# Attention heads of a fused decoder step: the rotated part of the scores on the two 64-row halves of the array by turns, a query tile's keys spread over two banks, no zero-padded key copies

## What is computed

```python
q = (c_q @ w_q_b).reshape(B, T, MLA_HEADS, QK_NOPE + QK_ROPE)      # 128 + 64 per head
q_pe = rope(q[..., QK_NOPE:], pos)
s = einsum('bqhc,bsc->bhqs', ql, c_kv) + einsum('bqhr,bsr->bhqs', qp, k_pe)
s = where(key_pos <= q_pos, s * ATTN_SCALE, NEG_INF)
p = softmax(s, axis=-1)
o = einsum('bhqs,bsc->bqhc', p, c_kv)
```

## Time and profile before

| | |
|---|---|
| runs of the kernel | 3501.75, 3492.95, 3504.45 us; median 3501.75 |
| the profiled execution | 3500.34 us, its span 3498.5 us |
| mean granted TensorE clock | 0.966 of full speed |
| TensorE busy in the array | 94% of the span, 26364 matmul records |
| weight loads | 84% |
| VectorE, ScalarE, GpSimd | 52%, 38%, 35% |

### The profile page before, as it was taken

One profiled execution on the slowest core, in us unless ns is written; L12 is line 12 of the kernel. 1 busy time (PEld: TensorE's weight loads), 2 busy tenths in 40 slices (PEclk: granted clock), 3 DMA queues, 4 the chain that ended last, 5 costly groups with the idle time before them and its releaser, 6 DMA issues.

```text
span 3498.5 us, 72361 instructions
## 1 busy us (share of the span) xinstructions
PE 3303.9 (94%) x26364; PEld 2948.1 (84%) x26364; DVE 1826.5 (52%) x3142; ACT 1345.1 (38%) x2810; POOL 1214.3 (35%) x847
## 2 busy tenths in 40 slices
PE   9999999999999999999999888888889999999998
PEld 6676766678899999997899877777778899999998
DVE  3454545213644377866203567666732464447785
ACT  2232323431454444322214455556521154453332
POOL 0000000010466677731223222223213066677771
PEclk9999999999999999999999989989978999999999
DMA  3121210630344554432223101100052045454442
GB/s 106 52 76 57 58 58 17 198 117 1 95 157 157 165 166 136 136 107 76 74 74 108 68 13 44 32 26 26 18 147 85 13 130 158 158 180 136 136 145 84
DMA packets 303577, 331.50 MB, mean 95 GB/s; under 512 B 54350, under 2 KB 285825, under 8 KB 303138
## 3 DMA queue, kind: packets, MB, share of 16 engines
q1 hardware_dynamic: 297346, 309.17, 27.9%
q0 software_dynamic: 6048, 19.73, 1.8%
HBM read 232.57 MB, written 116.69 MB: 100 GB/s over the span
## 4 chain that ended last, share of the span: by engine, by line
PE 60%; PEld 6%; DVE 5%; issue 4%; POOL 3%; ACT 2%; DMA 1%; SPq 0%; ACTq 0%; DVEq 0%; PEldq 0%; POOLq 0%
PE bank L615 58%; PEld bank L615 6%; PE bank L623 2%; POOL wloA L1953 1%; POOL arena L1953 1%; POOL wloS L1953 1%; DVE arena L3363 1%; DVE hT L3429 1%; SPq L1586 0%; ACT hT L2627 0%; DVE arena L3380 0%; DVE arena L2877 0%; DMA arena<-arena 0%; ACT arena L2177 0%; DVE arena L3067 0%
## 5 line engine op out<-in xcount | busy, mean ns | idle before, releaser
L615 PE MATMUL bank<-arena 128*128 128x268 f32 (+20 forms) x8302 | 1162.8, 333 | 77.9 <-ACT arena L2177 25.2
L615 PEld LDWEIGHTS bank<-arena 128*128 128x128 f32 (+7 forms) x8302 | 878.9, 178 | 339.7 <-issue 113.8
L1953 POOL TENSOR_TENSOR arena<-arena 128x512 f32<-128x512 f32 x120 | 165.7, 1381 | 1213.4 <-DMA arena<-in_ffn_w_up 766.9
L2177 ACT COPY arena<-bank 128x512 f32<-128x512 f32 (+14 forms) x557 | 252.6, 487 | 816.4 <-PE bank L615 590.9
L2357 ACT ACTIVATE whiS<-arena 128x512 fp32r<-128x512 f32 x180 | 113.0, 628 | 407.1 <-POOL arena L1953 393.9
L1953 POOL TENSOR_TENSOR wloA<-arena,whiA 128x512 fp32r<-128x512 f32 x180 | 262.4, 1471 | 0.4 <-ACT whiA L2354 0.4
L1953 POOL TENSOR_TENSOR wloS<-arena,whiS 128x512 fp32r<-128x512 f32 x180 | 238.9, 1341 | 49.1 <-ACT whiS L2357 49.1
L3229 DVE TENSOR_TENSOR hT<-hT,bank 128x536 f32<-128x536 f32 x280 | 197.4, 706 | 82.4 <-PE bank L615 82.0
L615 PE MATMUL bank<-hiT,whiS 128*128 128x268 f32 x768 | 199.9, 289 | 7.3 <-DVE loT L3071 3.7
L623 PE MATMUL bank<-table,arena 128*128 128x128 f32 (+5 forms) x1354 | 171.6, 268 | 26.1 <-DMA arena<-in_x_prompt 7.2
L3076 DVE TENSOR_TENSOR arena<-std,bank 128x268 f32<-128x268 f32 x192 | 80.4, 432 | 215.7 <-PE bank L615 209.3
(11 more groups left out here) (297 smaller groups left out, 8093.9 us busy)
## 6 DMA issues: line engine op xcount, KB each, us to landing
u_scratch<-arena SPq DMA_DIRECT2D x480, 134.0 KB, 1.8
arena<-in_ffn_w_up SPq DMA_DIRECT2D x64, 512.0 KB, 4.2
arena<-u_scratch SPq DMA_DIRECT2D x56, 536.0 KB, 5.1
arena<-in_ffn_w_down SPq DMA_DIRECT2D x112, 256.0 KB, 3.9
arena<-u_scratch SPq DMA_DIRECT2D x56, 402.0 KB, 6.0
arena<-past_scratch SPq DMA_DIRECT2D x32, 640.0 KB, 8.0
past_scratch<-in_cache_kv_latent SPq DMA_DIRECT2D x128, 128.0 KB, 2.4
past_scratch<-in_cache_k_rope SPq DMA_DIRECT2D x128, 32.0 KB, 2.1
```

The costliest lines, as they stand in the source:

```text
L615: return pe.matmul(out, lhsT, rhs, start=first, stop=last, skip_group_check=group)
L1953: return pool.tensor_tensor(out, a, b, op)
L2177: lane.do(act.copy(dst, b if view is None else view(b)), ring.drained)
```

## The change

The banks of a query tile are cut by a table, `SPLIT`: one bank for tiles 0 and 1, two of nearly the same number of key tiles for tiles 2 to 7, three for 8 and 9. That is 20 banks a head where there were 18. All banks of a tile first get the plain product over 128 rows. Then the rotated products follow over 64 rows: bank 0 (and bank 2 of tiles 8 and 9) on partitions 0 to 63, bank 1 on 64 to 127. With two banks each is cut in two parts and the halves take turns. The keys come from `kfull`; the queries of one half come from `qpe`, those of the other from a new copy `q_other` in which the two heads' halves are swapped. VectorE makes it in two copies each turn of the loop, after the plain keys of the pair's first head, and TensorE waits for it before that head's scores. `kz`, its zeros and its two copies go; the zeros in `qlat` are now written by VectorE.

```diff
--- before.py
+++ after.py
@@ -50,7 +50,8 @@
 
 Q_ORDER = [n // 2 if n % 2 else NQ - 1 - n // 2 for n in range(NQ)]
 ATT_A = sum(-(-(q + 1) // 4) for q in range(NQ))
-ATT_V = ATT_A + NQ
+SPLIT = [[q + 1] if q < 2 else [(q + 1) // 2, q + 1 - (q + 1) // 2] if q < 8 else [3, 3, q - 5] for q in range(NQ)]
+ATT_V = sum(len(s) for s in SPLIT) + NQ
 
 DVE_HEADS = 44
 DVE_CHUNK = 94
@@ -314,7 +315,8 @@
         qlat = m(3, DB, H * DS)
         olT = m(2, H, DB, DS)
         past_at = m.at
-        kz = m(2, T)
+        q_other = m(T)
+        m(T)
         cosT = m(T)
         sinT = m(T)
         wa = Carve(m.at)(KT, 768)
@@ -518,7 +520,7 @@
         in_s, rows_s, zero_s = sem("tables_loaded"), sem("rows_loaded"), sem("zeroed")
         sq_s, norm_s = sem("squares_ready"), sem("normed_ready")
         tile_s = [sem(f"tokens_loaded{t}") for t in range(NT)]
-        wa_s, rope_s, kz_s = sem("w_a_loaded"), sem("roped"), sem("kz_ready")
+        wa_s, rope_s, other_s = sem("w_a_loaded"), sem("roped"), sem("q_other_half")
         out_s, eps_s = sem("stored"), sem("eps_ready")
         wq_s, wq_used, wkv_used = sem("w_q_loaded"), sem("w_q_used"), sem("w_kv_used")
         max_s, exp_s, prob_s = sem("max_ready"), sem("exp_ready"), sem("probs_ready")
@@ -609,7 +611,7 @@
             ra = Fill(pe, BA, a_filled, a_drained)
             rv = Fill(pe, BV, v_filled, v_drained)
             sq_t, norm_t = Tally(sq_s), Tally(norm_s)
-            wq_t, wkv_t, prob_t = Tally(wq_s), Tally(wkv_used), Tally(prob_s)
+            wq_t, wkv_t, prob_t, other_t = Tally(wq_s), Tally(wkv_used), Tally(prob_s), Tally(other_s)
 
             def mm(out, lhsT, rhs, first, last, group=False):
                 return pe.matmul(out, lhsT, rhs, start=first, stop=last, skip_group_check=group)
@@ -749,6 +751,7 @@
                 prob_t.enter(i, 2 * NQ)
                 wq_t.enter(i, 64)
                 wkv_t.enter(i, 1)
+                other_t.enter(i, 2)
 
                 wq_t.expect(64)
                 pe.wait_ge(wq_s, wq_t.value())
@@ -782,13 +785,32 @@
                     if hh == 1:
                         wkv_t.add(pe.drain())
 
+                    if hh == 0:
+                        other_t.expect(2)
+                        pe.wait_ge(other_s, other_t.value())
+
+                    def roped(b, q, first, at, n, z):
+
+                        rows = slice(z * ROPE, (z + 1) * ROPE)
+                        return mm(b[0:QT, at * QT:(at + n) * QT], (qpe if z == hh else q_other)[rows, q * QT:(q + 1) * QT],
+                                  kfull[rows, (first + at) * QT:(first + at + n) * QT], False, True, True)
+
                     def scores(q):
-                        for j in range(0, q + 1, 4):
-                            n = min(4, q + 1 - j)
-                            b = rv.bank()
-                            mm(b[0:QT, 0:n * QT], qn[hh][:, q * QT:(q + 1) * QT], kn[hh][:, j * QT:(j + n) * QT], True, False)
-                            rv.done(mm(b[0:QT, 0:n * QT], qpe[:, q * QT:(q + 1) * QT], kz[:, hh, j * QT:(j + n) * QT],
-                                       False, True))
+                        firsts = [sum(SPLIT[q][:k]) for k in range(len(SPLIT[q]))]
+                        some = []
+                        for k, (j, n) in enumerate(zip(firsts, SPLIT[q])):
+                            b = rv.bank(ahead=k)
+                            mm(b[0:QT, 0:n * QT], qn[hh][:, q * QT:(q + 1) * QT], kn[hh][:, j * QT:(j + n) * QT], True, False, True)
+                            some.append(b)
+                        if len(some) != 2:
+                            for k, (j, n) in enumerate(zip(firsts, SPLIT[q])):
+                                rv.done(roped(some[k], q, j, 0, n, k % 2))
+                            return
+                        cuts = [[(0, n)] if n == 1 else [(n // 2 + n % 2, n // 2), (0, n // 2 + n % 2)] for n in SPLIT[q]]
+                        turns = [(z, cuts[z][back]) for back in (1, 0) for z in range(2) if back < len(cuts[z])]
+                        ends = [roped(some[z], q, firsts[z], at, n, z) for z, (at, n) in turns]
+                        for ins in ends[-2:]:
+                            rv.done(ins)
 
                     def turn_probs(n_):
                         q = Q_ORDER[n_]
@@ -822,6 +844,7 @@
                 prob_t.leave(4)
                 wq_t.leave(4)
                 wkv_t.leave(4)
+                other_t.leave(4)
             meet(pe, here)
 
             page_t = [[Tally(t) for t in four] for four in page_s]
@@ -1942,8 +1965,7 @@
         def _(pool):
             here = Tally(meet_s)
             pool.memset(rows_in[0:NROW, :], 0.0).then_inc(zero_s, 1)
-            pool.memset(kz[:, :, :], 0.0)
-            pool.memset(qlat[:, 2, :, :], 0.0).then_inc(kz_s, 1)
+            pass
             for _ in range(3):
                 meet(pool, here)
             def feed(layer):
@@ -2921,19 +2943,19 @@
 
             rope(kraw, kfull, kraw)
 
-            dve.wait_ge(kz_s, 1)
-            lane.do(dve.tensor_copy(kz[0:ROPE, 0, :], kfull[0:ROPE, :]))
-            lane.do(dve.tensor_copy(kz[ROPE:P, 1, :], kfull[ROPE:P, :]))
+            lane.do(dve.memset(qlat[:, 2, :, :], 0.0))
+            lane.settle()
             norm(ckv, ckv, 2, R_KVN, mark["norm_kv"])
             for p in range(3):
                 norm_piece(cq, cq, 3, R_QN, Tally(a_drained, mark["norm_q"][p]), *PIECES[p])
             meet(dve, here)
-            max_t, prob_t, exp_t = Tally(max_s), Tally(prob_s), Tally(exp_s)
+            max_t, prob_t, exp_t, other_t = Tally(max_s), Tally(prob_s), Tally(exp_s), Tally(other_s)
             with dve.Fori(0, H // 2) as i:
                 ring.drained.enter(i, 6 + 2 * (3 + ATT_V))
                 lane.order.enter(i, DVE_HEADS)
                 for t in (max_t, prob_t, exp_t):
                     t.enter(i, 2 * NQ)
+                other_t.enter(i, 2)
                 for at, w in PIECES:
                     take(qraw[:, at:at + w], P, w)
                 lane.settle()
@@ -2945,11 +2967,15 @@
                 for hh in range(2):
                     for at, w in PIECES:
                         take(kn[hh][:, at:at + w], P, w)
+                    if hh == 0:
+                        for z in range(2):
+                            there = slice((1 - z) * ROPE, (2 - z) * ROPE)
+                            other_t.add(dve.tensor_copy(q_other[there, 0:NP], qpe[z * ROPE:(z + 1) * ROPE, 0:NP]))
 
                     def maxima(n_):
                         q, pr, st = Q_ORDER[n_], probs[n_ % 3], stat[0:QT, n_ % 3]
-                        for j in range(0, q + 1, 4):
-                            n = min(4, q + 1 - j)
+                        for k, n in enumerate(SPLIT[q]):
+                            j = sum(SPLIT[q][:k])
                             b = ring.bank()
                             last = j + n == q + 1
                             if last:
```

## The result

The changed kernel takes 3507.05 us (median of 20 runs, 3500.51 to 3519.3); the kernel before, run beside it, 3500.48. The ratio is 1.0028, 95% interval [1.0019, 1.0037]. It isn't the quotient of the medians: they lie 7 us apart, and 1.0028 is 9.8 us. So the kernel is some 7 to 10 us slower. I had forecast 3500.4 us, no change.

A forecast was written before the change was run, and what follows sets the result against it. TensorE's queue was taken to bound the prompt's heads. Gains in six tiles less losses at tiles 9 and 1 gave -0.17 us a head, -1.4 in eight, so 3500.4 us; range 3489 to 3512.

The forecast's parts named there:

- my sum: Over the eight prompt heads: -0.36 + 0.14 + 0.05 = -0.17 us a head, -1.4 us in all.
- the six tiles without waits: Scores of query tiles 7, 2, 6, 3, 5, 4: 2.62 us saved, 2.26 paid for switches, 0.36 won per head.
- widths: Unit of score work on TensorE: 104 keys of one matmul, 0.175 us; the six tiles save 15 per head.
- The halves run in pairs: Rotated scores: 64-row products on the two partition halves run at once, at full pace, as in the second layer.
- A change of mode costs: Switching between 128-row and 64-row matmuls drains the array: in 0.18, out 0.195, together 0.375 us a query tile.
- Two more banks are free on TensorE: 128-row part of each head, 20 banks for 18: two more matmuls at about 0.01 us, counted as nothing.
- the added wait and copies are covered: Before a turn's first scores: VectorE's copies done 5 us early, cost 0; uncovered 6 us.
- tile 9's chain: VectorE's copies, mask and maximum before a head's first transposes: the wait ends 0.14 us later per head.
- the stretch with tile 1: Tile 1's scores save no width; 0.23 us of cover before value products leaves 0.05 us lost per head.
- the price of two halves: Section pricing the entry to and exit from 64-row matmuls: 0.375 us a tile, 30 us for 80 tiles.
- part by part: List of effects in the heads, on VectorE and ahead of the loop; all beyond the heads' score tiles counted 0.
- The rival "slower": In the six tiles without waits the unequal halves don't run together: 20 us lost, 3521 us; chance 0.1.

The follow-up runs named there:

- one_half: Changed kernel with every 64-row product on partitions 0 to 63, so no two run at once: 3537.62 us, 1.0115 of the kernel before.
- banks_only: Changed kernel with its new banks and order, but rotated products over 128 rows with zero-padded keys as before: 3508.20 us, 1.0021 of the kernel before.
- after_pad: Changed kernel plus 34 tiny matmuls behind the heads, moving later code to 255 instructions further than before: 3498.15 us, 1.0 of the kernel before.
- after_again: Changed kernel, unedited, measured and profiled a second time: 3505.65 us, 1.0019 of the kernel before.
- after_fill: Changed kernel plus one unneeded 416-column matmul ahead of each of four waits a head: 3496.22 us, 0.9986 of the kernel before.
- before_pad: Kernel before plus 29 tiny matmuls behind the heads, moving later code 117 instructions further: 3506.64 us, 1.0025 of the kernel before.
- before_pad_again: Kernel before with the same 29 tiny matmuls (117 instructions further), run once more: 3505.41 us, 1.0019 of the kernel before.
- before_pad_far: Kernel before with 64 tiny matmuls in place of 29, later code 257 instructions further: 3505.59 us, 1.0011 of the kernel before.
- after_fill_pad: Changed kernel with the four filling matmuls a head plus 26 tiny matmuls behind the heads, 257 instructions further: 3485.74 us, 0.9961 of the kernel before.
- before_fill: Kernel before plus one unneeded 416-column matmul ahead of each of four waits a head: 3491.61 us, 0.9974 of the unedited one.

## Why the prediction was wrong

The measured 3507.05 us lies inside my range of 3489 to 3512, but above the 3497 to 3504 that I gave 0.72, and the kernel became slower where my sum had it 1.4 us faster.

Right, by its own steps:

- *TensorE's queue bounds the stage, and only the six tiles without waits pay.* Their 20.74 us became 20.42, for -0.36 forecast; each tile came out within 0.04 us of widths x 0.175 less 0.375, so the price of a switch in and out holds.
- *The halves run in pairs.* one_half pays 6.2 us a turn without them.
- *A change of mode costs.* The table shows it in tile 2, that saves one width, 0.175, and still is 0.22 longer, so 0.395 for in and out. The rule of the Trainium skill on this (TensorEngine Tiling (Array Packing), Key Properties: a change of mode drains the array) agrees with the trace, here with a price.
- *Two more banks are free on TensorE, the added wait and copies are covered.* In banks_only the six tiles take 20.75 us for 20.74; in the changed kernel the stretch with tile 1 grew by 0.02 for 0.05.

Wrong in size: tile 9's chain. I let the transposes come 0.14 us later; they come 0.05 earlier, though the wait in front of them grew by 0.14 (7.0 to 8.1 us in eight heads). TensorE came to it 0.18 us earlier, and VectorE was no later. The two parts of this show in banks_only: the banks that fill together, without the halves, bring the transposes 0.22 us later, and the halves by turns give 0.27 back. My 0.14 was meant for both together. With -0.05 in place of +0.14 the sum is -0.36 a head, -2.9 in the loop, as it came out.

**The step that failed** is one that the sum didn't have. Outside the heads I put the change at nothing, because no work was added there: "the price of two halves" and the list "part by part" counted instructions as time on an engine, not as length of a program. The 118 instructions that the change adds to TensorE's program move all later code, and in this kernel as many instructions are worth some 6 to 9 us. Added without the change they make the kernel before as slow (3506.64, 3505.41); 137 more on top of the change bring the changed kernel level with the one before (3498.15). In the traces the changed kernel loses 4.3 to 6.9 us in two turns of a loop that the change doesn't touch. The rival "slower" named unpaired halves at 3521 us; that was not it, and my chance of 0.12 for a time over 3512 us held no mechanism for this one.

What is shown and what isn't:

- Shown: the time depends on how many instructions lie between the heads and the later code, by adding some to either kernel. And shown for the changed kernel: 4.3 to 6.9 us of the 10 to 13 lie in the chunk loop (303.8 and 303.9 us for 299.5 and 297.0), and they go when that loop is moved on (296.2), which is all of what after_pad gains.
- Shown for the changed kernels alone: a second stop behind each return of the chunk loop, 1.9 us in all in after_again and 4.8 in after_fill, gone in after_pad. That it is a fetch of code is argued from the packets' times and from the branch, which takes 3.3 to 3.9 us when it returns and 0.08 when it leaves. The 1.9 us don't make the loss, but the clock goes with them: in the two turns both profiles of the changed kernel have 58.0 us at half clock, those of before 51.2 and 47.8, after_pad 44.4. By the price of a half-clock stretch (4.5 us for 10.2) the 8.5 us more than the mean of before are an estimate of 3.8 us; 1.9 + 3.8 is 5.7, and the means of the turns differ by 5.6. Whether the stops bring these falls about wasn't tried. The mean clocks over all runs don't show it: after_again is 0.0014 under the kernel before beside it, after_pad 0.0011.
- Open: the rest of the changed kernel's 10 to 13 us. Also open: where the kernel before loses most of its 6 to 9 us when it is padded. Its mean clock is 0.0009 lower in before_pad and no lower in before_pad_again, and there is no second stop. So that its loss has the same mechanism as the changed kernel's isn't shown. It isn't shown either how much of after_pad's gain is work in the wait ahead of the sample stage.
- The worth of the change itself is to be read where the later code lies at the same place with it and without. It is between nothing and a small gain. Near 117 further: 1.0028 and 1.0019 with it, 1.0025 and 1.0019 without, the same. Near 256: 1.0 [0.9987, 1.0012] (after_pad) with it, 1.0011 [0.9999, 1.0024] (before_pad_far) without. With filled waits, at unlike places (257 and 34) and on different chips: after_fill_pad 0.9961, before_fill 0.9974. The 2.8 us of the loop are within all of these but resolved by none.

## What to carry to other kernels

Two 64-row halves by turns pay only when a group saves more than its switch (here 0.375 to 0.395 us, over two widths of 104 keys), and only where TensorE isn't waiting. Where an edit is worth a few us of some thousand, shift the later code of the longest program by a dummy of a hundred instructions or so and measure this too, before the edit is praised or blamed. In a tuned kernel look at the clock behind short waits that follow each other closely: useless work of the waits' length was worth more here than the change (before_fill 0.26%; the changed kernel 1.0019 to 0.9986).

## What was unexpected of the hardware

- TensorE's later code moved on by 117 instructions, with nothing else changed: +8.6 and +6.3 us. By 257: 1.0011 [0.9999, 1.0024]. The changed kernel moved from 118 to 255 further: 1.0028 and 1.0019 became 1.0.
- The branch at the end of the second layer's chunk loop takes TensorE 3.3 to 3.9 us when it returns and 0.08 us when it leaves; that of the heads' loop takes at most 0.25 us.
- At a return of the second layer's loop TensorE stands for 1.5 to 2.2 us for nothing but "issue", and in some placements once more, 0.7 to 2.6 us, some 3 us later.
- At the end of some heads TensorE's clock goes to 1.2 GHz for 10.2 us, 4.5 us lost each, though the engine only waited twice shortly before, for 0.67 and 0.73 us. In the kernel before, which heads it strikes differs from one execution to the next. With a matmul in each of these waits there was none between the loop's start and the last head's end in before_fill.
